# Layer-2 mixers: who builds the decay matrices, and how the delta rule's state is laid out

## The reference, cut to what matters

```python
def lower_exp_diff(cs):
    diff = cs[..., :, None] - cs[..., None, :]
    return jnp.where(tril, jnp.exp(jnp.where(tril, diff, 0.0)), 0.0)

# SSD: xc = xs * dt
scores = einsum('bclhn,bcshn->bhcls', cc, bc) * lower_exp_diff(a_cs)
y_diag = einsum('bhcls,bcshp->bclhp', scores, xc)
chunk_states = einsum('bclhn,bhcl,bclhp->bchpn', bc, decay_states, xc)
state = state * chunk_decay + chunk_states

# GDN, chunk by chunk (u, w come from a triangular solve with k.k * lower_exp_diff(gc))
v_new = u_i - einsum('bhld,bhde->bhle', w_i, state)
o = einsum(q_i * exp(g_i), state) + einsum(qk_i, v_new)       # qk = q.k * lower_exp_diff(gc)
state = state * exp(g_last) + einsum(k_i * exp(g_last - g_i), v_new)
```

## Time and profile before

| what | us |
|---|---|
| median of 3 runs | 2253.35 |
| lowest, highest | 2251.65, 2255.38 |
| span of the profiled execution | 2258.5 |
| PE busy in it | 2216.4 |
| DVE busy | 1581.9 |
| ACT busy | 914.2 |
| POOL busy | 263.5 |

### The profile page before, as it was taken

The page is one execution under the profiler, slowest core; times in us unless marked ns, Lnnn a source line. Parts: engine busy times, 40 slices in busy tenths (PEclk is TensorE's granted clock), DMA queues, the critical chain, the costliest instruction groups (busy, mean ns, idle before and its releaser), DMA issues. The chain is left out here.

```text
span 2258.5 us, 34288 instructions
## 1 busy us (share of the span) xinstructions
PE 2216.4 (98%) x13052; PEld 1823.0 (81%) x13052; DVE 1581.9 (70%) x2212; ACT 914.2 (40%) x1672; POOL 263.5 (12%) x266
## 2 busy tenths in 40 slices
PE   8999999999999999999999989999999999999997
PEld 7888888888888887887877777887888888888886
DVE  5657678876665545657687788887798777765557
ACT  5443544343343321243344445555533333324444
POOL 0222232100000000001232222322020000000000
PEclk9999999999999999999999989999999999999999
DMA  4111111144333264433233442323235444448655
GB/s 152 47 38 58 37 56 38 66 147 157 116 114 111 86 261 175 150 111 122 85 112 112 150 141 72 107 93 112 96 131 191 163 158 163 158 156 299 214 181 184
DMA packets 106952, 289.06 MB, mean 128 GB/s; under 512 B 9692, under 2 KB 35388, under 8 KB 102332
## 3 DMA queue, kind: packets, MB, share of 16 engines
q1 hardware_dynamic: 106812, 287.14, 36.2%
HBM read 205.01 MB, written 82.10 MB: 127 GB/s over the span
## 5 line engine op out<-in xcount | busy, mean ns | idle before, releaser
L124 PE MATMUL psG<-h_hi,w_hi 128*128 128x512 f32 (+1 forms) x624 | 164.4, 395 | 2.1 <-DVE features_T L1875 1.6
L124 PE MATMUL psG<-h_hi,w_lo 128*128 128x512 f32 (+1 forms) x624 | 161.6, 391 | 0.0
L124 PE MATMUL psG<-h_lo,w_hi 128*128 128x512 f32 (+1 forms) x624 | 161.4, 392 | 0.0
L455 POOL TENSOR_TENSOR sb_w<-sb_left 128x128 f32<-128x128 f32 (+3 forms) x96 | 96.9, 1014 | 320.3 <-DVE sb_left L582 320.3
L124 PEld LDWEIGHTS psG<-h_hi,w_hi 128*128 128x128 f32 x624 | 109.9, 188 | 23.7 <-DVE features_T L1875 2.9
L124 PEld LDWEIGHTS psG<-h_hi,w_lo 128*128 128x128 f32 x624 | 111.4, 188 | 20.2 <-DVE w_lo L155 0.2
L124 PEld LDWEIGHTS psG<-h_lo,w_hi 128*128 128x128 f32 x624 | 111.1, 188 | 20.1 <-issue 0.5
L582 DVE TENSOR_TENSOR_SCAN sb_left<-sb_left 128x128 f32<-128x128 f32 (+3 forms) x96 | 102.7, 1078 | 2.1 <-ACT sb_left L468 1.4
L150 ACT CAST w_hi<-w_raw 128x1024 fp32r<-128x1024 f32 x48 | 50.3, 1049 | 120.0 <-PE psG L124 61.7
L155 DVE TENSOR_TENSOR w_lo<-w_raw,w_hi 128x1024 fp32r<-128x1024 f32 x48 | 58.6, 1222 | 55.0 <-ACT w_hi L150 55.0
L2024 POOL TENSOR_TENSOR features_T<-m_bias_both 128x512 f32<-128x512 f32 x10 | 16.8, 1675 | 680.3 <-DMA m_bias_both<-in_proj_pairs 633.0
(11 more groups left out here) (657 smaller groups left out, 5949.8 us busy)
## 6 DMA issues: line engine op xcount, KB each, us to landing
w_raw<-in_units SPq DMA_DIRECT2D x76, 512.0 KB, 4.3
w_raw<-hidden_blocks SPq DMA_DIRECT2D x77, 256.0 KB, 2.9
merge_gates<-features_T SPq DMA_DIRECT2D x12, 1024.0 KB, 6.7
merge_gates<-merge_gates SPq DMA_DIRECT2D x12, 1024.0 KB, 4.8
features<-features_T SPq DMA_DIRECT2D x24, 512.0 KB, 3.8
w_spare<-in_units SPq DMA_DIRECT2D x22, 512.0 KB, 4.4
down_sums<-w_spare SPq DMA_DIRECT2D x22, 512.0 KB, 3.3
hidden_blocks<-features_T SPq DMA_DIRECT2D x11, 1024.0 KB, 3.9
```

What stands on the lines that cost most here:

```text
L124: return pe.matmul(out, lhs, rhs, start=first, stop=last, skip_group_check=True)
L455: pool.tensor_tensor(w, left_chunk(S, 1), left_chunk(S), ALU.subtract).then_inc(w_ready, 1)
```

## The change

Four parts. (1) The mask: `dsub` and `dmask` leave DVE; POOL makes `nac`, the negative of each token's sum (128 x 12), and adds the mask to DEC (`dm`, 128 x 1536) between keep1 and xd. (2) The exponentials: twelve, one for each head, with `nac` as the bias, GDN's heads first (`LG`), then SSD's (`LS`); from n=1 on they stand behind `product(8)` and so ahead of `high_weights`, `moved` and `product(16)`; nc, nt and qkd wait for LG, sd for LS. (3) xdt, xdec and st1 go to POOL: the first two behind xd, st1 between nm and vbt, where it waits for yo and for the last st2; POOL's par waits for att in place of st1. (4) The state is 128 x 2 x 64 without the zero blocks: two updates in place of four, and in vn and o the product with 128 rows is replaced by two with the 64 rows of each head. The outputs of one parity share a bank (`chain_out`), vn and o use the same place, and so `level_t(2)` waits for og.

```diff
-        QKDC, QGT, S = l[9].take("qkd_chain", [P, GH, P]), l[10].take("qgt", [P, 2, P]), l[10].take("gdn_state", [P, 2, P])
+        QKDC, QGT, S = l[9].take("qkd_chain", [P, GH, P]), l[10].take("qgt", [P, 2, P]), l[10].take("gdn_state", [P, 2, 64])
+        chain_out = lambda h: PS[:, 5 + h % 2, 256 + 64 * (h // 2):320 + 64 * (h // 2)]
@@ sync
-            vectX.wait(sp, "xdt", LAST)
-            poolF.wait(sp, "xd", LAST)
+            vectF.wait(sp, "sd1", LAST)
+            poolF.wait(sp, "xdt", LAST)
@@ gpsimd
-                    vectF.wait_last(g, "st1", n)
+                    vectF.wait_last(g, "att", n)
                     poolF.done("par", g.tensor_copy(PT[:], prm[:, n, :]))
+                    poolF.done("nac", g.tensor_tensor(NAC[:], zero[:].to_broadcast([P, NH]), prm[:, n, PACS:PACS + NH], ALU.subtract))
...
                     poolF.done("keep1", copy(g, AQK[:], F[:, AQ0:AQ0 + 3, :], zero))
+                    g.wait_ge(dec_here, 16 * n + 16)
+                    poolF.done("dm", g.tensor_tensor(DEC[:], DEC[:], over(MSK[:, 0, :], NH), ALU.add))
...
+                    tensF.wait_last(g, "stn", n)
+                    poolF.wait(g, "par", n)
+                    poolF.done("xdt", g.tensor_tensor(heads(XDT[:], SH), heads(XS[:], SH), per(PT[:, PDT:PDT + SH], SH, 64), ALU.mult))
+                    poolF.wait(g, "xdt", n)
+                    poolF.done("xdec", g.tensor_tensor(heads(XDE[:], SH), heads(XDT[:], SH), per(PT[:, PED:PED + SH], SH, 64), ALU.mult))
...
+                    tensY.wait(g, "yo", n)
+                    vectF.wait_last(g, "st2", n)
+                    poolF.done("st1", g.tensor_tensor(heads(ST[:], SH), heads(ST[:], SH), per(PT[:, PET:PET + SH], SH, 64), ALU.mult))
@@ scalar, behind product(8)
+                    poolF.wait(a, "dm", n)
+                    for h in (*range(SH, NH), *range(SH)):
+                        ins = a.activation(DEC[:, h], DEC[:, h], ACT.Exp, bias=NAC[:, h:h + 1])
@@ scalar, behind upper()
-                    vectF.wait(a, "dmask", n)
-                    scalL.done("L", a.activation(DEC[:], DEC[:], ACT.Exp))
@@ vector
-                    vectF.done("dsub", tt(DEC[:], DEC[:], per(PT[:, PACS:PACS + NH], NH, P), ALU.subtract))
-                    vectF.wait(v, "dsub", n)
-                    vectF.done("dmask", v.scalar_tensor_tensor(DEC[:], DEC[:], 0.0, over(MSK[:, 0, :], NH), ALU.min, ALU.add))
...
-                        for h in range(GH):
-                            m, r = h // 2, half(h)
-                            vectD.done(f"s{h}", v.scalar_tensor_tensor(S[r, m, r], S[r, m, r], PSC[r, m:m + 1],
-                                                                       PS[r, 4, 64 * m:64 * m + 64], ALU.mult, ALU.add))
+                        for m in range(2):
+                            vectD.done(f"s{m}", v.scalar_tensor_tensor(S[:, m], S[:, m], PSC[:, m:m + 1],
+                                                                       PS[:, 4, 64 * m:64 * m + 64], ALU.mult, ALU.add))
@@ tensor
                     if b == 2:
-                        scalG.wait_last(pe, "vn", i)
+                        vectG.wait_last(pe, "og", i)
...
                     for m in range(2):
-                        mm(PS[:, 5, 256 + P * m:256 + P * m + P], WT[:, m], S[:, m], True, False)
                         for h in (2 * m, 2 * m + 1):
-                            x = mm(PS[:, 5, 256 + 64 * h:256 + 64 * h + 64], VT[:, h], VBT[:, 64 * h:64 * h + 64], False, True)
+                            mm(chain_out(h), WT[half(h), m], S[half(h), m], True, False)
+                        for h in (2 * m, 2 * m + 1):
+                            x = mm(chain_out(h), VT[:, h], VBT[:, 64 * h:64 * h + 64], False, True)
...
-                        mm(PS[:, 6, P * m:P * m + P], QGT[:, m], S[:, m], True, False)
+                            mm(chain_out(h), QGT[half(h), m], S[half(h), m], True, False)
```

## The result

The changed kernel takes 2290.70 us in the median of 4 runs (2289.15 to 2292.46), against 2252.53 for the kernel before in the same comparison (2251.65 to 2255.38): 38 us more, a ratio of 1.0164 with an interval of 1.0150 to 1.0179. The forecast was 2261.5. The direction was right, the size was not, and the time lies above the range that ended at 2267. The profiled span of after is 2290.7, that of before 2258.5, so 32 us of the 38 can be looked for in the two traces; the other 6 are how far the profiled execution of before lay above its median.

A forecast was written before the change was run, and what follows sets the result against it. PE was taken to bound the steady tiles, DVE and the clock n=1. Terms 8.2 + 1.6 + 1.85 - 2.8 - 0.6 = +8.2 us on 2253.35 gave 2261.5 us, +0.36%; range 2250 to 2267.

The forecast's parts named there:

- the 1.59 of the earlier trace: GpSimd step of 256 elements beside other work, used to set dm's upper end at 4.5 us.
- the 5 that were to show the forecast right: Sign in steady tiles from n=3 on: DVE's busy time down by some 5 us a tile.
- The shape's price: PE's vn and o: 64-row products cost 0.34 us a pass, +1.36 a chain, +8.2 for six chains.
- The tail's term: Last chain (i=7), between products of 512 columns: 0.06 a pass added by estimate, +1.6 us.
- The doubling in n=1: Chain i=0 runs at half clock, so its 1.36 costs somewhat less than twice: +1.85 us.
- n=1 and n=2: First tiles: mask and exponential leave the way to X64; -2.8 us in n=1, -0.6 in n=2.
- The exponentials: ACT's twelve take 0.21 to 0.30 each, fit idle time or delay T16's copy: 0, at most 1 us over all tiles.
- A: Rival: PE's change of shape costs nothing; faster or even, 2249 to 2250 us; chance 0.10.
- B: Rival: clock stays at 1.00 through n=1, worth -9.6 us; even, some 2252 us; chance 0.22.
- C: Rival: POOL's mask is late, PE waits 1 us in six tiles; 2267 us; chance 0.18 with similar delays.
- that view: What PE's loads wait for in four steady tiles: read as gaps up to 0.4 us, nearly all without releaser, no engine waited for.

The follow-up runs named there:

- 5: Changed kernel with the same dm instruction, for the next tile, moved ahead of vbt, where DVE idles: 2275.42 us, ratio 1.0105 to the kernel before.
- 6: As 5, with GpSimd's xd, xdt and xdec also waiting until VectorE is done with qg: 2274.78 us, ratio 1.0097 to the kernel before.
- 7: As 6, with the old state (with zero blocks) restored: 2263.45 us, ratio 1.0042 to the kernel before, period 35.52.
- 8: As 7, with SSD's eight exponentials moved ahead of the wt copy: 2261.47 us, ratio 1.0029 to the kernel before, period 35.18.
- 1: Kernel before with only the state without zero blocks and its products of vn and o: 2268.01 us for 2256.10, ratio 1.0056.
- experiment 3: Changed kernel with the state with zero blocks restored, all else as changed: 2279.01 us, ratio 1.0106 to the kernel before.
- experiment 9: Changed kernel with dm at its old place but cut into twelve instructions of 128x128: 2283.37 us, ratio 1.0130 to the kernel before.
- 2: As 1, with the 64-row products of all four heads together, two borders in and out a chain, not four: 2258.50 us for 2254.24, ratio 1.0015.

## Why the prediction was wrong

**Where the 32 us of the two traces are.** vn's first load stands at 1344.38 in n=1 (1341.72 before): +2.7. n=2 adds 2.4 (1386.34, before 1381.32), the five tiles n=3 to 7 add 24.9, some 5 each, the tail 1.3, the end of the kernel 1. A steady tile's 4.95 divide, by the experiments, into 3.09 for dm's place (after to 5), 0.38 for xdt and xdec (5 to 6), 0.33 for the exponentials ahead of `moved` (7 to 8) and 1.14 for the state's shape (1): 4.94. The parts hold in this order only: with dm at its old place, the old state alone gave back 1.7 to 1.9 (experiment 3). The direction was right, and for a reason that was forecast, but the shape is some 9 us of the 38.

**The step that failed** is "POOL gains `dm`, xdt, xdec, st1 ... still in POOL's 23.8 idle us: hidden, 0." Each term of that was near: dm takes 3.46 (forecast 3.0 to 3.3, at most 4.5), it ends ahead of ScalarE's need, and nobody waits for it. What was wrong is the word hidden. I asked what DVE's work does to GpSimd's (the 1.59 of the earlier trace rows) and not what GpSimd's does to DVE's, and I took idle time on GpSimd to be free. For the same reason DVE's busy time fell by 0.4 us a tile (29.41 for 29.82) and not by the 5 that were to show the forecast right: a step that stands still counts as busy. The trace of before had the sign, in rows that I did not set side by side. DVE's ysc and GpSimd's copy of m_bc in tile n=6 of before:

```profile
1498.43 0.36 DVE L2797 TENSOR_SCALAR small_cols<-small_cols 128x2 f32<-128x2 f32 x1
...
1497.73 1.04 POOL L119 TENSOR_TENSOR m_bc<-m_feat,m_zero 128x512 f32<-128x512 f32 x1
```

ysc took 0.36, 0.17 when nothing ran beside it (experiment 5), and it ended at 1498.79, 0.02 behind the copy. With DVE 5.4 us idle in a tile I looked for no path on it at all; but ysc releases ScalarE's yln, behind which the z, ga and T4 copies queue, and PE waits for T4 2.35 us a tile.
The Trainium skill states this outright, on the page SBUF — State Buffer, section Who interferes with whom: GpSimd's only SBUF ports are DVE's second pair, held for a whole instruction, against DVE instructions with two SBUF inputs (when GpSimd's reads SBUF) and against those in its two-port modes; one SBUF input outside those modes, and reductions, do not contend. The traces agree on the kinds of step: the steps that stood still are additions, products and a scaling between SBUF tiles, while a reduction kept its 0.67 beside dm (experiment 3) and nt and qkd, with one input from PSUM, their 0.69 and 0.68 beside nm. On how long a step is held they go further than the page: in one tile of experiment 9 ysc stood for five of GpSimd's instructions in a row, not for one. I cited two other pages in the prediction and not this one, which spoke against the change.

**The shape's price** was right in kind and a little high: 1.15 a chain for 1.36, as the border measured 0.15 wherever 64-column products stand beside it. The tail's term measured 1.3 for 1.6; the 0.06 a pass that I added there came from no row that I named, and 0.33 a pass was measured for 0.29 in a steady tile. The doubling in n=1 did not occur, since the chain there ran at a clock of 1.00.

**n=1 and n=2** were forecast at -2.8 and -0.6 and came out at +2.7 and +2.4. The exponential left its place, as said, but dm and xd stopped DVE's steps for 4 us at 1317 to 1322, earlier in the same tile, where DVE sets the pace, and again for 3.8 in n=2. PE's idle time grew by some 3 us from the stage's start to vn of n=1 and by 3.5 from there to vn of n=2, while its busy time fell by 0.3 and 1.1, so these losses are waits and not the clock.

**The exponentials** took the upper end, 0.30 each, and delayed not T16 but the copy ahead of it; 0.33 a tile against a bound of 1 us in all.

**The rivals.** A fell (experiments 1 and 2). B came half true, the clock's low stretch moved out of n=1's chain, and it brought little, because it moved into the run-up: PE's busy time up to vn of n=2 fell by 1.4 us, where B had 9.6. C named the right instruction with the wrong mechanism. My reading of the earlier trace rows was loose as well: beside the 12.8 us without a releaser that view has 4.7 that name DVE or ScalarE, in gaps of at most 0.4. The rival that was missing is the one that decided: GpSimd as the cause of a stall, not as its victim.

## What to carry to other kernels

Idle time on GpSimd is not free time: before a step is moved there, list the VectorE instructions that will run beside it, and ask of each whether all its inputs lie in SBUF and who waits for it. The same instruction cost 3.1 us a steady tile at one place and nothing at another, where VectorE was waiting anyway. The halved products saved nothing on TensorE here, since each pass added two changes of shape, 0.15 us each: four passes a chain lost 1.14 us, two passes 0.57; with the zeros left in there is no such price.

## What the runs showed that I had not expected

A VectorE step of two elements for each partition took 3.2 us beside one GpSimd instruction of 128x1536, and was let go 0.03 us behind its end. Cutting that instruction into twelve did not always help: the engines took turns in four steady tiles, and in the fifth VectorE waited until the last of the twelve was done.
